# Two-block network on one core: layer normalisation's tile sums moved to VectorE, the second group of recurrent heads two steps later, the last product by quarter blocks

## The reference, cut to what matters

```python
def layer_norm(x, g, b):            # over 1024 channels, used in conv_branch and in sgu_branch
    xc = xf - jnp.mean(xf, axis=-1, keepdims=True)
    var = jnp.mean(xc * xc, axis=-1, keepdims=True)
    return xc * lax.rsqrt(var + EPS) * g + b
...
def cd_layer(h, ...):
    u, qd, fd, idd, gate = jnp.split(h @ w_in, CD_SPLIT, axis=-1)
    yc = s5_mixer(u, ...)                       # ends in y * sigmoid(y @ w_glu + b_glu)
    f = lower_bound + (1.0 - lower_bound) * sigmoid(fd)
    od = chunked_gated_linear_attention(silu(qd), 1.0 - f, idd, log(f))    # 8 heads of 128
    yd = head_rmsnorm(od, hgrn_norm_g)
    y = jnp.concatenate([yc, yd], axis=-1) * jax.nn.silu(gate)
    return y @ w_out                            # 256 x 2048 times 2048 x 2048
...
return rmsnorm(h + cd_layer(...), final_g)
```

## Time and profile before

| what | value |
|---|---|
| median of 3 runs | 3223.94 us (3222.12 to 3227.08) |
| the profiled execution's own time | 3222.26 us |
| its span | 3220.3 us |
| mean granted TensorE clock | 0.982 |
| TensorE busy | 3151.1 us |
| VectorE busy | 1685.5 us |
| ScalarE busy | 339.5 us |
| DMA, mean over the span | 170 GB/s |

### The profile page before, as it was taken

One profiled execution on the slowest core, in us unless ns is written; L12 is line 12 of the kernel. 1 busy time (PEld: TensorE's weight loads), 2 busy tenths in 40 slices (PEclk: granted clock), 3 DMA queues, 4 the chain that ended last, 5 costly groups with the idle time before them and its releaser, 6 DMA issues.

```text
span 3220.3 us, 46341 instructions
## 1 busy us (share of the span) xinstructions
PE 3151.1 (98%) x20412; PEld 2769.7 (86%) x20412; DVE 1685.5 (52%) x2624; ACT 339.5 (11%) x640; POOL 60.5 (2%) x116
## 2 busy tenths in 40 slices
PE   5899999999999999999999999999999999999998
PEld 2588855478889999999999999989988898898887
DVE  1247635422216577766666777853321265996632
ACT  1110000013230000011110000001012102000010
POOL 0000000020000000000000000000000000000000
PEclk8899998999999999999999999999999999999999
DMA  8986755674445555755555555555455554553353
GB/s 342 351 273 208 233 186 197 247 183 118 128 121 157 179 160 161 178 169 173 158 171 160 168 171 170 163 138 145 112 139 143 144 171 125 150 145 107 103 145 116
DMA packets 675027, 547.95 MB, mean 170 GB/s; under 512 B 23909, under 2 KB 656320, under 8 KB 662029
## 3 DMA queue, kind: packets, MB, share of 16 engines
q1 hardware_dynamic: 646656, 467.69, 49.0%
q0 software_dynamic: 10832, 70.41, 5.9%
q10 hardware_dynamic: 17341, 6.90, 0.9%
HBM read 542.75 MB, written 2.22 MB: 169 GB/s over the span
## 4 chain that ended last, share of the span: by engine, by line
PE 94%; DMA 3%; DVE 2%; ACTq 0%; issue 0%; ACT 0%; DVEq 0%; POOLq 0%
PE psum L424 45%; PE psum L456 11%; PE psum L445 8%; PE psum L517 5%; PE psum L797 2%; PE psum L796 2%; PE psum L787 2%; PE psum L790 2%; PE psum L483 2%; PE psum L785 2%; PE psum L795 2%; PE psum L782 2%; DMA ring<-w_mod 2%; DMA arena<-w_mod 1%; PE psum L840 1%; PE psum L667 1%
## 5 line engine op out<-in xcount | busy, mean ns | idle before, releaser
L424 PE MATMUL psum<-arena,ring 128*128 128x256 f32 (+2 forms) x6400 | 1469.6, 390 | 9.2 <-DVE arena L1990 7.2
L424 PEld LDWEIGHTS psum<-arena,ring 128*128 128x128 f32 x6400 | 1215.0, 191 | 242.4 <-issue 85.1
L456 PE MATMUL psum<-arena 128*128 128x128 f32 x3200 | 365.5, 275 | 0.0
L456 PEld LDWEIGHTS psum<-arena 128*128 128x128 f32 x3200 | 361.3, 192 | 0.0
L445 PE MATMUL psum<-arena,ring 128*128 128x128 f32 x2400 | 276.3, 275 | 0.0
L445 PEld LDWEIGHTS psum<-arena,ring 128*128 128x128 f32 x2400 | 272.2, 192 | 0.2
L1730 DVE SCALAR_TENSOR_TENSOR arena<-arena,cvec 128x2048 f32<-128x2048 f32 x60 | 141.1, 2351 | 140.3 <-DMA arena<-w_mod 139.4
L1593 DVE TENSOR_TENSOR arena<-ring 128x2048 f32<-128x2048 f32 x50 | 114.6, 2292 | 173.4 <-PE psum L456 173.2
L517 PE MATMUL psum<-ring,arena 128*128 128x128 f32 x1536 | 173.3, 275 | 0.0
L517 PEld LDWEIGHTS psum<-ring,arena 128*128 128x128 f32 x1536 | 172.5, 192 | 0.5 <-issue 0.4
L2306 DVE TENSOR_TENSOR arena<-ring 128x1024 f32<-128x1024 f32 x64 | 78.4, 1225 | 90.0 <-PE psum L782 89.1
(11 more groups left out here) (305 smaller groups left out, 2821.0 us busy)
## 6 DMA issues: line engine op xcount, KB each, us to landing
ring<-w_ff SPq DMA_DIRECT2D x128, 1024.0 KB, 5.9
ring<-w_in SPq DMA_DIRECT2D x104, 1024.0 KB, 5.9
arena<-w_mod POOLq DMA_DIRECT2D x64, 1024.0 KB, 7.0
ring<-ab_w_in SPq DMA_DIRECT2D x56, 1024.0 KB, 5.4
ring<-cd_w_in SPq DMA_DIRECT2D x48, 1024.0 KB, 5.8
ring<-w_mod SPq DMA_DIRECT2D x32, 1024.0 KB, 6.7
ring<-w_o SPq DMA_DIRECT2D x16, 1024.0 KB, 5.6
ring<-ab_w_out SPq DMA_DIRECT2D x16, 1024.0 KB, 5.9
```

What stands on the lines that cost most here:

```text
L424: mm = pe.matmul(psum[:, s, m * N:(m + 1) * N], w[:, k, m * P:(m + 1) * P], x(k)[:, 0:N], start=(j == 0), stop=(j == kt - 1))
L456: mm = pe.matmul(o, tb[:, i, j, :], x(t, j), start=(j == 0), stop=(j == HT - 1))
```

## The change

Three edits in one kernel.

- The 8 tiles of `ZV`, `CV` and of their squares are added up on VectorE, by one `tensor_reduce` each over the tile index (`tile_sums`), into one tile; TensorE then multiplies that one tile by ones. Both `ZV` and `CV` are added up at once, ahead of the first three chunks.
- The second group of recurrent heads comes two steps (one slot) later, its last sums at step 35 in place of 33.
- Of `cd_out`'s 16 output tiles, 12 are done as 6 pairs by quarter blocks; the first two and the last two stay plain. The input sums are made after the gating, and the finished tiles are transposed two at a time inside a pair, from the second pair on.

```diff
-    ("cd_out", "cd_w_out_2", 0, 4, 16, 128),
+    ("cd_out", "cd_w_out_2", 0, 4, 32, 128),
...
-RECUR_VALUES = {9: 0, 11: 1, 13: 2, 15: 3, 23: 4, 25: 5, 29: 6, 31: 7}
-RECUR_SCORES = {6 + u: u for u in range(8)} | {20 + u: 8 + u for u in range(4)} | {26 + u: 12 + u for u in range(4)}
-RECUR_SUMS = {18: 0, 33: 1}
+RECUR_VALUES = {9: 0, 11: 1, 13: 2, 15: 3, 25: 4, 27: 5, 31: 6, 33: 7}
+RECUR_SCORES = {6 + u: u for u in range(8)} | {22 + u: 8 + u for u in range(4)} | {28 + u: 12 + u for u in range(4)}
+RECUR_SUMS = {18: 0, 35: 1}
...
+        TC, SC3 = at(20480, 4, HT, P), [at(24576 + 1024 * i, HT, P) for i in range(4)]
...
+                        elif kt == 32:
+                            q = 4 * i + s
+                            if 2 <= q < 14:
+                                c = q // 2 * 2 * width
+                                load(w[:, 8 * (q % 2):8 * (q % 2) + 8, c:c + 2 * width], s, 2 * width)
+                            else:
+                                load(w[:, :, q * width:(q + 1) * width], s, width)
...
             def beside_k(q):
                 if q == 0:
                     pe.wait_ge(sem("ln_in"), n["ln_in"].next())
-                    sum_rows(ZV, 4, "dve", HT)
+                    sum_rows(TOTAL, 4, "dve", 1)
                 elif q == 1:
                     pe.wait_ge(sem("squares_ready"), n["squares_ready"].next())
-                    sum_rows(SQ, 5, "dve", HT)
+                    sum_rows(TOTAL, 5, "dve", 1)
...
-            for q in range(16):
-                one_slot("cd_out", lambda k: Y5P[:, k, :] if k < HT else YD[:, k - HT, :], "dve", q % 4,
-                         order=(*range(HT, KT), *range(HT)), before=both_gated if q == 0 else None)
-                if q > 0:
-                    turn_result(q - 1)
+            def ahead(p):
+                turn_result(2 * p - 4)
+                turn_result(2 * p - 3)
+
+            for q in range(2):
+                one_slot("cd_out", both, "dve", q, order=(*range(HT, KT), *range(HT)),
+                         before=both_gated if q == 0 else None)
+            pe.wait_ge(sem("input_sums"), n["input_sums"].next())
+            for p in range(1, 7):
+                pair(p, both_quarters, TC, mid=None if p == 1 else (lambda p=p: ahead(p)), first=1)
+            for q in range(14, 16):
+                one_slot("cd_out", both, "dve", q % 4, mid=(lambda: ahead(7)) if q == 14 else None)
+                if q == 15:
+                    turn_result(12)
+                    turn_result(13)
+                    turn_result(14)
             turn_result(15)
...
+            def tile_sums(x, name, total=TOTAL):
+                v.tensor_reduce(total[:, 0, :], x.rearrange("p k t -> p t k"), AX_X, ALU.add).then_inc(
+                    sem(name), n[name].up())
+                v.wait_ge(sem(name), n[name].now())
+
             def layer_norm_sums(z, sq):
-                v.sem_inc(sem("ln_in"), n["ln_in"].up())
                 def centre():
...
-                    v.tensor_tensor(sq, z, z, ALU.mult).then_inc(sem("squares_ready"), n["squares_ready"].up())
+                    TT(sq, z, z, ALU.mult)
+                    tile_sums(sq, "squares_ready")
...
             v.wait_ge(sem("uv_ready"), n["uv_ready"].next())
+            tile_sums(ZV, "ln_in")
+            tile_sums(CV, "ln_in", TOTAL2)
             centre = layer_norm_sums(ZV, SQ)
             chunk = chunks(3)
...
             no_squares()
-            for k in range(KT):
+            for half in range(2):
+                x = (Y5P, YD)[half]
+                quarter_sums(x, [z[:, 4 * half:4 * half + 4, :] for z in SC3], "input_sums" if half else "vector_step")
...
+            for k in range(2):
+                add_in(k, k)
+                result(k)
+            fast[0] -= 1
+            w = pair_differences("cd_out", 1, TC, ahead=False)
+            pair_sums(1, w, TC, ahead=False)
+            for k in range(2):
+                square(X[:, k, :])
+            for p in range(1, 7):
+                if p < 6:
+                    w = pair_differences("cd_out", p + 1, TC)
+                    pair_sums(p + 1, w, TC)
+                pairs_added(p)
+                for k in (2 * p, 2 * p + 1):
+                    i = 4 * (p % 2) + 2 * (k % 2)
+                    TT(X[:, k, :], X[:, k, :], STAGE[:, i:i + 2, :].rearrange("p a t -> p (a t)"), ALU.add)
+                    result(k)
+                for k in (2 * p, 2 * p + 1):
+                    square(X[:, k, :])
+            for k in range(14, KT):
                 add_in(k, k % 4)
-                gained(U4[:, k, :], k, col("final_g_2", k), "result_tile")
+                result(k)
                 square(X[:, k, :])
```

More of the change, by code:

```diff
@@ L190, in program @@
         RS, MEAN, TMP = at(40688, T), at(40944, T), at(41200, 2, T)
+        TOTAL, TOTAL2 = at(41200, 1, T), at(41456, 1, T)
         SGB = at(41712, P)
@@ L433, in quarters, with pair @@
                 return ring[:, s, :].rearrange("p (i f m c) -> p i f m c", f=2, m=2, c=P)[:, :, f, m]
-            def pair(p, x, tb, mid=None):
+            def pair(p, x, tb, mid=None, first=0):
                 a, b, s0 = 2 * (p % 2), 2 * (p % 2) + 1, 2 * (p % 2)
@@ L446, in pair @@
                                        stop=(j == HT - 1))
-                        if p == 0 and t == j == 0:
+                        if p == first and t == j == 0:
                             leave(mm, s0)
@@ L643, in beside_k @@
                     pe.wait_ge(sem("ln_in"), n["ln_in"].next())
[L644 removed]
+                    sum_rows(TOTAL2, 4, "dve", 1)
                 elif q == 6:
                     pe.wait_ge(sem("squares_ready"), n["squares_ready"].next())
[L647 removed]
+                    sum_rows(TOTAL, 5, "dve", 1)
             def modulated(k):
@@ L1583, in loaded, with pair_differences @@
                     v.wait_ge(sem(f"load_slot{q % 4}"), n[f"load_slot{q % 4}"].now())
-            def pair_differences(name, p, tb):
+            def pair_differences(name, p, tb, ahead=True):
                 loaded(first_slot(name) + 2 * p, 2)
-                if p >= 1:
+                if p >= 1 and ahead:
                     n["differences_used"].n = fast[0] + p
@@ L1596, in pair_differences, with pair_sums @@
                 return w
-            def pair_sums(p, w, tb):
-                if p >= 1:
+            def pair_sums(p, w, tb, ahead=True):
+                if p >= 1 and ahead:
                     v.wait_ge(sem(full("dve", 2 - s_of(p))), n[full("dve", 2 - s_of(p))].now(1))
                 TT(tb[:, 2], w[:, :, 1, 1], tb[:, 0], ALU.subtract)
-                if p >= 1:
+                if p >= 1 and ahead:
                     v.wait_ge(sem(full("dve", 3 - s_of(p))), n[full("dve", 3 - s_of(p))].now(1))
@@ L2695, in recur_done @@
                 TT(heads(g), heads(g), GATE3[:, HT + 4 * g:HT + 4 * g + 4, :], ALU.mult)
-            for t in range(6, 34):
+            for t in range(6, 36):
                 if t in RECUR_VALUES:
@@ L2706, in _ @@
                     levels(HG, 1)
-                elif t == 23:
+                elif t == 25:
                     recur_done(0)
-                elif t == 31:
+                elif t == 33:
                     head_squares(squares(1), heads(1))
@@ L2721, in _, with result @@
             no_squares()
-            for k in range(KT):
+            for half in range(2):
+                x = (Y5P, YD)[half]
+                quarter_sums(x, [z[:, 4 * half:4 * half + 4, :] for z in SC3], "input_sums" if half else "vector_step")
+            def result(k):
+                gained(U4[:, k, :], k, col("final_g_2", k), "result_tile")
+            for k in range(2):
[18 more added lines that the diff above has]
+            for k in range(14, KT):
                 add_in(k, k % 4)
-                gained(U4[:, k, :], k, col("final_g_2", k), "result_tile")
+                result(k)
                 square(X[:, k, :])
```

6 lines of the change are left out of this document (4 added, 2 removed).

## The result

The change runs in 3203.77 us (median of 4 runs, 3200.46 to 3208.16) against 3224.76 of the kernel before beside it: a ratio of 0.9936, 95% interval 0.9919 to 0.9953, or 21.0 us. On another chip it gave 0.9929 (0.9916 to 0.9943). I had forecast 3198.1 us, a gain of 24.2. The profiled execution took 3205.22 us, with a span of 3203.2.

A forecast was written before the change was run, and what follows sets the result against it. TensorE, busy 98% of the span, was taken to bound the kernel. Tile sums 9.3, heads 7.0 and last product 7.9 us sum to 24.2 us off 3222.26, giving 3198.1 us, with a range of 3189 to 3208.

The forecast's parts named there:

- Four sums at 3.02 us: Tile sums: one tile in place of 8 cuts each TensorE sum from 3.45 to 0.43 us, 12.1 us in all.
- The reduce at 3.9 us: VectorE's tile sums: each strided tensor_reduce of 2048 elements costs 3.9 us, between 2.3 and 8.4.
- the first rival: Tile sums: the reduce costs only a plain instruction's 2.3 us, TensorE waits 1.2, total 3196.5 us; chance 8%.
- The wait at 2.8 us: Stage k: TensorE waits 2.8 us for the reduce of CV's squares, leaving part 1 a gain of 9.3 us.
- TensorE ends slot 5 at 518.67: Stage k: the starting time from which TensorE reaches the sum of CV's squares at 532.8, before VectorE's 535.6.
- The half-clock stretch: Stage k: the new 2.8 us wait might cost a half-clock stretch like the old one's 2.2 us, giving 3200 us.
- The wait of 0.68 us at the end of `v` stays: End of stage v: TensorE's wait behind the last sixteen w_mod chunks stays at 0.68 us.
- Their chain moves along: Stage v: the last sixteen w_mod chunks start when TensorE has left MACC, so they move along with it.
- my sign of being wrong: The forecast is wrong if TensorE waits in stage v, at the start of the last product, or in every pair.
- the clock falls elsewhere: Near 485 to 510 us: a shift could spare TensorE's half-clock loss, up to 9 us, giving 3189 us; chance 4%.
- The cover at the end of glu: End of glu: the second group is gated at 3086.6, 1.7 us before TensorE ends glu at 3088.3.
- The rival that ended slower: Last product: VectorE and TensorE alternate, a pair costs 22.1 us against 13.82, total 3256 us; chance 3%.

The follow-up runs named there:

- p1_sums_only: The kernel before with only the tile sums moved to VectorE: 3216.94 us, ratio 0.9976.
- change_again: The change itself run a second time, unaltered: 3204.88 us, ratio 0.9929 against the kernel before.
- reduce_in_rows: The change with each tensor_reduce adding 8 neighbouring elements of a row, so wrong sums and no step: 3208.31 us, one run.
- p2_heads_only: The kernel before with only the second group of recurrent heads one slot later: 3218.4 us, ratio 0.9973.
- p3_blocks_only: The kernel before with only the last product by quarter blocks: 3219.68 us, ratio 0.998.
- late_again: Second run of the change with the row sum of CV's squares taken after slot 7 of stage k, not slot 6: 3198.48 us, ratio 0.9911.
- tree_late: The change with three adds replacing each tensor_reduce and the second sum of squares one slot later: 3197.55 us, ratio 0.991.

## Why the prediction was right, and where it wasn't

**The direction and the size.** 21.0 and 21.4 us against 24.2. From slot 0 of "k" to the end the profiled executions gave 21.5 us.

**Part 1, the tile sums: the right mechanism, with two slips that cancelled by luck and a stretch that scatters.** Forecast 9.3. The four kernels without tile sums need 261.8 us on average from slot 0 of "k" to the end of "v" (261.4 to 262.2). The four with the change's code there need 255.3, 257.4, 250.4 and 249.6, mean 253.2: 8.7 us gained on average, between 4.5 and 12.3 in single executions. Of the 8.7, 9.8 are won up to the third row sum of w_mod, where both the saved sums and the wait lie and for which I had 9.3, and 1.1 are lost behind it. My terms:
- Four sums at 3.02 us: in the profile 0.43 us each from start to start, as worked out.
- The reduce at 3.9 us: 3.6. The estimate from the strided rows was near, and the first rival (2.3 us, 8%) was wrong. The Trainium skill's rule on cachelines (SBUF — State Buffer, Specifications) holds in direction: with a step each access is in a new line, and the same instruction took 2.29 us in rows and 3.6 with the step. By the tier table of the Trainium skill (VectorE: DVE Perf Modes) the reduce stands with the plain instruction; that holds for the reduce in rows and not for the stepped one.
- The wait at 2.8 us: 4.01 in the change's profile, 2.4 on average. The step that failed is "TensorE ends slot 5 at 518.67": the two sums already removed by then, 6 us, are missing in it. With them, and `centre` held fixed at 526.60 as I did, the wait would have come to 8.8 us. That 2.8 came out near is luck: the second slip went the other way, since `centre` moves forward too. It follows chunks that follow VectorE's products with TensorE's results, and these come earlier as TensorE does: `centre` starts at 519.52 in p1_sums_only, though slot 0 ended 2 us later than before. The lead of 7.93 us is what stays on average (7.87), and it varies with the loads and with the clock in slot 5 between 6.53 and 9.58. The change's own 4.01 us lay outside the 1 to 3 us that I had named as the sign in the profile.
- The half-clock stretch, which I left in my range: 1.17 - 0.59 and 15.16 - 13.90, 1.8 us, in one profile of four.
- "The wait of 0.68 us at the end of `v` stays": 0.35 in the change, 3.16 in change_again, 3.75 in reduce_in_rows, 0.72 or less in the others where the row shows it. With the kernels of before it was 0.41 to 0.98. "Their chain moves along" held, since the chunks start behind the third row sum in every profile; that TensorE's own time to the end of the chain is fixed did not. So my sign of being wrong, a wait in stage "v", does not show in the change's first profile and does in its second, at 4.1 us and through the chunks' loads and the clock, not through a gain that is paid back.
- The clock ahead of all this: from slot 0 to the sum of `CV` the removal of two sums should leave 104.9 - 6.0 = 98.8 us. The table has 98.7, but also 100.6 and twice 96.5. That is the rival "the clock falls elsewhere", in both directions and at 2 us; I had put up to 9 on it. Of the 4.1 us between 100.6 (change_again) and 96.5 (p1_sums_only), 2.6 arise ahead of the small matmuls, where the row sum of w_mod took 4.01 us for 3.63 and the slot behind it 15.11 for 13.90, and 1.5 behind their start.

**Part 2, the heads: right in each term.** 7.0 us between the end of step 20 (22) and the end of glu, 7.2 in p2_heads_only behind stage "v". The wait of 4.83 us and the half clock are gone. The cover at the end of glu, forecast at 1.7 us, measured 2.2.

**Part 3, quarter blocks: right.** 7.8 us for 7.9; p3_blocks_only 7.9. The wait of pair 1 was 0.27 us for 0.4, pairs 12.94 us with their transposes, and the final wait fell from 1.02 to 0.58 us. The rival that ended slower, VectorE and TensorE in turns, needed 4 us of wait in each pair; behind the first there was none.

**What stays open.** Median against median the change wins some 2.5 us less than the profiles' means give (8.7 + 7.2 + 7.9 = 23.8). The start's scatter could hold it. No run tells. Nor do the runs settle how much of the 6.4 us between late_again and change_again is the later slot's: from slot 0 of "k" to the end of "v" the three profiles with it need 251.1, 246.0 and 251.6 us, mean 249.6, against 253.2 for the change's code, and their ranges overlap. Why the clock falls at one place in one execution and at another in the next isn't shown either.

## What to carry to other kernels

Moving a sum from the engine that bounds to one with time to spare wins the bounding engine's time only if the result is asked for late enough; price the wait by the lead between two engines, which stays near its size when both move, and not at absolute times. A lead that hangs on DMA landings and on the clock varies: leave a slot of slack rather than a microsecond. And compare one code over several profiles before a difference of 2 to 5 us is put down to an edit; here the same code gave waits of 1.5 to 4.0 us.

## What was unexpected

- TensorE's clock after an idle stretch. Behind idle stretches of 1.12, 1.37, 1.52, 1.71 and 2.45 us the next slot ran at the upper level (13.90 us, or 3.62 for half a slot of gate_cd), behind 4.01 and 4.83 us part of it ran at the lower. So the wait of 4.01 us cost 5.8 in all, and the one of 2.45 cost 2.45. But the length of the wait does not decide it. The kernel has three more waits for VectorE outside the edits, the same to 0.01 us in all fourteen profiles: behind that of 2.70 us near 1300 us the lower level followed in eleven (8.88 us for 7.20), behind that of 2.30 near 2120 in twelve (15.74 for 14.05), behind that of 2.25 near 2665 in two (8.83 for 7.15). The same wait costs 1.7 us more in one execution than in another. The waits of 3.16 and 3.75 us at the last row sum of w_mod had the lower level behind them too (5.80 and 6.50 us for 3.73), but there the clock isn't a sign of the wait alone: tree_late has 4.76 us and p1_sums_only 5.03 for the same row sum with no wait at all.
- The clock falls beside the edits too, and not at the same place each time. In the series of small matmuls of stage "k", busy time by stretch (columns as above), first late_again, then change_again, each from 80 us behind the end of its slot 0:

```profile
493.23:501.23 8.00, 8.00 (x15) 3.47 (x15) 5.12 (x3) 0.00 (x0) 1.06 (x2) 0.68 0.58 202
```

```profile
499.54:507.54 8.00, 8.00 (x17) 4.59 (x18) 3.97 (x4) 0.00 (x0) 0.26 (x1) 0.50 0.09 17
```

  late_again is further on at this point: it was through the series sooner, with less of its slot 4 and of the series at the lower level. TensorE never idled there: all 8 us are busy in both.
- A `tensor_reduce` of 2048 elements with a step of 1 KB costs 1.6 times one in rows (3.6 against 2.29 us), and three plain adds that halve the tile cost 2.4 us, a third less than the stepped reduce.
